# A feed-forward's element-wise work and the halves of the next weights, in the other order

## The reference

```
def swiglu(h, w_gate, w_up, w_down):
    return (jax.nn.silu(h @ w_gate) * (h @ w_up)) @ w_down

# in second_block, for each layer i:
    x = layer_norm(ALPHA * x + (1.0 + g_m) * y, ln_mix_g[i], ln_mix_b[i])
    h = x * (1.0 + sc_f) + sh_f
    y = swiglu(h, w_gate[i], w_up[i], w_down[i])
    x = layer_norm(ALPHA * x + (1.0 + g_f) * y, ln_ffn_g[i], ln_ffn_b[i])
```

## Time and profile before

| | |
|---|---|
| time, median of 3 runs | 3062.44 us |
| time of the profiled execution | 3062.7 us |
| its span, first to last instruction | 3061.0 us |
| TensorE busy | 2720.3 us, 89% |
| VectorE busy | 1507.5 us, 49% |
| ScalarE busy | 1080.4 us, 35% |
| mean granted clock of TensorE | 0.932 of full speed |

### The profile page before, as it was taken

How to read it: one execution, slowest core, us unless ns; L and a number is a source line. 1 busy time by engine, 2 the same in 40 slices (tenths; PEclk the granted TensorE clock), 3 DMA queues, 4 the chain that set the end, 5 groups by cost and what they waited for, 6 DMA issues and landing times.

```text
span 3061.0 us, 30785 instructions
## 1 busy us (share of the span) xinstructions
PE 2720.3 (89%) x12303; PEld 2068.2 (68%) x12303; DVE 1507.5 (49%) x2270; ACT 1080.4 (35%) x1606; POOL 9.7 (0%) x30
## 2 busy tenths in 40 slices
PE   4896689999989899999797978899997998799997
PEld 4661167778776577878685646778776774678785
DVE  3339747464635446455534464423336474623235
ACT  3330134232444433233424643422225463422223
POOL 0000000000000000000000000000000000000000
PEclk8979989999999999999897888999998997899998
DMA  3219723233222123323231002223222210233231
GB/s 121 83 69 367 278 55 97 83 96 87 93 76 70 42 69 96 97 86 87 76 87 55 1 1 55 69 83 96 83 83 83 56 56 14 69 97 94 74 101 49
DMA packets 326267, 262.61 MB, mean 86 GB/s; under 512 B 15433, under 2 KB 315234, under 8 KB 326126
## 3 DMA queue, kind: packets, MB, share of 16 engines
q1 hardware_dynamic: 324762, 257.34, 27.1%
q0 software_dynamic: 992, 3.17, 0.3%
q10 hardware_dynamic: 372, 0.14, 0.0%
HBM read 258.50 MB, written 2.12 MB: 85 GB/s over the span
## 4 chain that ended last, share of the span: by engine, by line
PE 79%; DVE 10%; ACT 5%; issue 2%; DVEq 2%; PEld 1%; PEldq 1%; ACTq 0%; SPq 0%; DMA 0%
PE ps L362 52%; PE ps L380 6%; PE ps L376 6%; PE ps L384 6%; DVE y L1692 3%; DVE wL L328 2%; PE ps L1247 2%; ACT wH L314 1%; PE ps L1278 1%; PE ps L1261 1%; ACT tmpB L1319 1%; PEld ps L2017 1%; PE ps L867 1%; DVEq L1694 1%; PE ps L1813 1%
## 5 line engine op out<-in xcount | busy, mean ns | idle before, releaser
L328 DVE TENSOR_TENSOR wL<-raw,wH 128x2048 fp32r<-128x2048 f32 (+1 forms) x186 | 416.1, 2237 | 997.6 <-ACT wH L314 996.8
L314 ACT ACTIVATE wH<-raw 128x2048 fp32r<-128x2048 f32 (+1 forms) x186 | 348.1, 1871 | 1128.1 <-PE ps L362 796.4
L362 PE MATMUL ps<-hH,wH 128*128 128x512 f32 (+1 forms) x1656 | 425.0, 399 | 0.0
L362 PE MATMUL ps<-hL,wH 128*128 128x512 f32 (+1 forms) x1656 | 421.9, 397 | 0.0
L362 PE MATMUL ps<-hH,wL 128*128 128x512 f32 (+1 forms) x1656 | 420.9, 396 | 0.0
L362 PEld LDWEIGHTS ps<-hH,wH 128*128 128x128 f32 x1656 | 311.3, 190 | 76.4 <-issue 2.9
L362 PEld LDWEIGHTS ps<-hL,wH 128*128 128x128 f32 x1656 | 310.1, 189 | 74.9 <-issue 1.2
L362 PEld LDWEIGHTS ps<-hH,wL 128*128 128x128 f32 x1656 | 309.2, 188 | 74.2 <-issue 1.0
L376 PE MATMUL ps<-gH,wH 128*128 128x512 f32 x480 | 158.8, 418 | 19.4 <-ACT wH L314 18.5
L380 PE MATMUL ps<-gH,wL 128*128 128x512 f32 x480 | 156.9, 413 | 10.7 <-DVE wL L328 10.7
L376 PE MATMUL ps<-hH,wH 128*128 128x512 f32 (+1 forms) x272 | 93.9, 439 | 48.0 <-ACT hH L988 31.2
(11 more groups left out here) (331 smaller groups left out, 3327.5 us busy)
## 6 DMA issues: line engine op xcount, KB each, us to landing
raw<-w_up SPq DMA_DIRECT2D x132, 512.0 KB, 5.2
mod_ring<-w_mod SPq DMA_DIRECT2D x64, 768.0 KB, 6.5
raw<-w_down SPq DMA_DIRECT2D x32, 1024.0 KB, 5.1
raw<-w_gate SPq DMA_DIRECT2D x44, 512.0 KB, 4.0
raw<-w_down SPq DMA_DIRECT2D x16, 768.0 KB, 4.5
raw<-w_in_even SPq DMA_DIRECT2D x9, 1024.0 KB, 5.1
raw<-w_out SPq DMA_DIRECT2D x8, 1024.0 KB, 5.4
raw<-w_in_odd SPq DMA_DIRECT2D x16, 512.0 KB, 5.1
```

What stands on the lines that cost most here:

```text
L314: last = act.activation(wH[:, st.slot, 0:st.size], raw[:, st.slot, 0:st.size], ACT.Copy)
L328: last = dve.tensor_tensor(wL[:, st.slot, 0:st.size], raw[:, st.slot, 0:st.size], wH[:, st.slot, 0:st.size].bitcast(F32), ALU.subtract)
L362: last = pe.matmul(dst, left, right, start=(t == 0 and k == 0), stop=(t == 2 and k == self.kt - 1))
```

## The change

In `scalar_plain` and `vector_plain` the halves of strip n+2 move from the head of the loop over strips to its end. For each up strip, ScalarE now does silu, `gH`, and then `wH` of the strip two ahead; VectorE does the product, `gL`, and then `wL`. Nothing else is changed: loads, TensorE's order, and the halves in other stages stay.

```
             def scalar_plain(self, act):
                 for s, st in self.numbered():
-                    split_high(act, st.n + 2)
-
                     act.wait_ge(ff_prod.sem, self.prod0 + s - 1)
                     act.wait_ge(tile_done.sem, st.tiles[0].done)
                     act.activation(tmpB[:, s % 2, :], ps[:, st.tiles[0].bank, :], ACT.Silu).then_inc(ff_silu.sem, 1)
                     act.wait_ge(ff_prod.sem, self.prod0 + s + 1)
                     act.activation(gH[:, s, :], ff_tmp[:, s % 2, :], ACT.Copy).then_inc(ff_high.sem, 1)
+                    split_high(act, st.n + 2)
 
             def vector_plain(self, dve):
                 for s, st in self.numbered():
                     gate_in, value = st.tiles
-                    split_low(dve, st.n + 2)
                     dve.wait_ge(tile_done.sem, value.done)
                     dve.wait_ge(ff_silu.sem, self.silu0 + s + 1)
                     dve.sem_inc(bank_read[gate_in.bank].sem, 1)
                     dve.tensor_tensor(ff_tmp[:, s % 2, :], ps[:, value.bank, :], tmpB[:, s % 2, :], ALU.mult).then_inc(ff_prod.sem, 1)
                     dve.drain().then_inc(bank_read[value.bank].sem, 1)
                     self.low(dve, s)
+                    split_low(dve, st.n + 2)
```

## The result

The changed kernel takes 3078.92 us (median of 5 runs, 3077.85 to 3087.74) against 3065.87 us for the kernel before on the same chip (5 runs, 3061.46 to 3068.79). The ratio is 1.0052, with a 95% interval of 1.0034 to 1.0070. Measured once more on another occasion, the ratio was 1.0047 (1.0034 to 1.0060), 3078.81 against 3062.81 us. It is slower by about half a percent, and the forecast was 3077. The profiled execution has a span of 3077.1 us, 16.1 more than before, and a mean granted clock of 0.929.

The account below looks back on a forecast made before the run. TensorE was taken to bound the kernel, with 79% of the span through it; VectorE and ScalarE cost only where it stands still. 8.7 + 1.6 + 0 + 4.7 = 15.0 us on 3062.4 gives 3077.4, range 3069 to 3085.

Parts of the forecast that it names:

- (1): Six up-to-down transitions: the second down strip's high-half copy starts 1.45 us later behind gH, 8.7 us in all (7.5 to 8.9).
- first waits: TensorE's waits for the second down strip's high half wH at six transitions: 3.1 us at four, 2.7 at two.
- second waits: TensorE's waits for the second down strip's low half at the six transitions: still 1.07 and 0.54 us.
- (2): Start of each gated feed-forward: a new wait of 0.80 us for strip 2's high half, 1.6 us for two.
- (3): Strips in the middle of an up product: copies 1.45 us later, but 9.06 us of slack, so cost 0.
- (4): TensorE's clock behind the transitions: one half-rate stretch of about 1.5 us each, + 4.7 us (0 to + 11.9).
- Rival A: Waits at transitions and entries grow, but the clock doesn't follow: 3072.7 us; chance 0.22.
- B: Clock falls for two stretches or more at most transitions, + 9 to + 11.9 us: about 3083 us; chance 0.12.
- C: Steady strips pay too, as loads or halves come late: 43.5 us more than the forecast, 3121; chance 0.02.
- D: Transitions really hang on the last strip's gH and gL, which come earlier, so both waits go: 3043.5 us; chance 0.02.
- E: No change within the measurement: the clock gives back elsewhere what is lost, some 10 us; chance 0.04.

## Why the prediction was right

(1) **The transitions' waits.** I had 1.45 us each, 8.7 in all; it is 1.32 in the long ones, 1.34 and 1.69 in the short ones, 8.3. The steps: product's start at V + 0.18 in five of six (I took 0.30, between bounds of 0.10 and 0.33), then 0.73 (0.72) and 0.53 (0.53). Only the first was unknown in the trace of before, and the whole difference is there. The nearest row had said 0.24; to go above it, on the thought that the increment would cost more here, was the wrong direction. The sixth transition, at V + 0.53, is outside my bounds, for a reason that stays open; it brought the sum nearer to the 8.7 by chance. The first waits were to be 3.1 and 2.7 and are 3.01 (3.02 once), 2.59 and 2.94. The second waits were to stay at 1.07 and 0.54. They did in the second, third and fifth transition; in the first, fourth and sixth they are 0.19, 0.73 and none, since slow matmuls filled the time. That the copy's place is the cause is shown from three sides: take gH out of its way and nothing is lost, keep the change for the last strips alone and the full waits are there, take away the need for D1 and the cost at the transitions goes.

(2) **The entries.** 0.80 us each expected, 0.69 and 0.70 measured between the same points; the rows show 0.50 and 0.49, as an idle time is some 0.2 shorter than the step that it causes. The product again followed faster (0.14 behind the silu).

(3) **The steady strips** cost nothing: 112.45 against 112.46 us, and the trace has no wait in the middle of an up product.

(4) **The clock.** I had + 4.7 and it is + 6.3, inside the bounds of 0 and 11.9. The idea of one stretch of 1.5 us behind each transition was too simple: it costs between 0.65 (the sixth) and 2.8. It was luck that the term came this near: with the same six waits the clock's part was 1.8 in another kernel. Rival A (no more clock) was nearer to that kernel than my forecast would have been. What the clock does elsewhere could have moved the time by as much: executions of the kernel before alone range from 3054 to 3072 us. Sum: 8.3 + 1.4 + 6.3 = 16.0 against 15.0.

Of the rivals, B wanted some 2.7 us of clock at most transitions; only the second and the fourth, at 2.78 and 2.35, come near it. C and D fell with (3) and with the waits still for wH and wL. E, too: behind the changed stages the clock gave back 1.3 us, not 10.

**A page's rule.** The Trainium skill, "TensorE: Matmul & The Clock Gate", Terms, puts the penalty at half the time at half rate. In the three stretches of the first transition the clock is 0.91, 0.50 and 0.53 over 3.0, 3.0 and 3.5 us, that is 0.5 + 3.0 + 3.3 = 6.8 us at half rate, and by that rule 3.4 us. The transition's clock part is 1.89. So the rule is an upper bound here, as in the trace before: the slow matmuls ahead of the second wait ran into time that would have been idle (that wait is 0.19 in place of 1.07, so 0.88 us cost nothing), which leaves 2.5. The other 0.6 us isn't placed; some of the half-rate time lies in the waits themselves.

## What to carry to other kernels

An engine's queue is in order, so whatever is moved behind a waiting instruction inherits its wait. Before moving a weight's preparation, look for the one strip per loop that is wanted at once; all the others may have 9 us of slack and still the few decide. And where a product interleaves two strips from its first matmul, see whether the first strip can be done alone for some microseconds: here that took out 53 us, while none of the orders of the preparing work that were run gained anything. When an effect is a few microseconds, compare the waits in the traces first. The first waits here repeat to some 0.02 us wherever the order of the work is the same, while the clock moves the total by several microseconds in code that is the same.

## What the runs showed of the hardware

TensorE's clock fell to 1.2 GHz around all six first waits of 2.6 to 3.0 us in the changed kernel (with the last strips alone changed, the third, 2.58 us, stayed at full clock: 20.47 us) and at most places behind 1.7 (three of four in the kernel before). Filling the wait with matmuls that nobody needs held the granted clock at 1.00, which is 2.4 GHz, at all six transitions: 72 more of them took 10.6 us off the changed kernel's transitions, and 36 took 4.3 us off those of the kernel before. The ratio to the kernel before went from 1.005 to 1.000 in the one and was 0.9974 in the other. The clock's price of one and the same wait ranged from 0 to 1.5 us (1.69 + 1.07 us; 2.7 for the product at 440 us in the kernel before, 28.41 against 25.74) and from 0.6 to 2.8 (3.01 + 1.07) from place to place. In two executions of the changed kernel that took the same time within 0.1 us, each transition repeated to 0.03 us.

A VectorE product that waits for a TensorE tile started 0.18 us behind the tile's end at five places, with a semaphore increment queued between, and 0.53 us at a sixth; behind a ScalarE silu it took 0.14.
